# Attention in pairs of heads with one rotary query tile, and the rotary angles two normalisations later

## Chip, cores and metric

One core of one Trainium2 chip runs the whole block once, in float32. The metric is the device time in microseconds of one execution; three executions of the kernel before took 2652.34, 2653.70 and 2655.47 us, median 2653.7.

## What is computed

One decoder block over 2048 tokens of width 1024, cut to what the change touches:

```python
ang = positions[..., None] * inv_freq                 # 32 frequencies
cos, sin = jnp.cos(ang), jnp.sin(ang)
h = rms_norm(x, norm_w) * (1 + scale) + shift         # scale, shift from c @ w_ada
a_val, a_glu, a_gate, cq, ckv, k_pe, b_gate, g_a, g_b = split(h @ w_in)
# convolution branch on a_val, a_glu, a_gate -> y_a
q  = (rms_norm(cq, q_norm_w) @ w_uq).reshape(s, 8, 128 + 64)   # per head: nope, rope
kv = (rms_norm(ckv, kv_norm_w) @ w_ukv).reshape(s, 8, 128 + 128)
q_rope = apply_rope(q[..., 128:], cos, sin)           # [x1*cos - x2*sin, x1*sin + x2*cos]
k_rope = apply_rope(k_pe, cos, sin)                   # one for all heads
scores = (q_nope @ k_nope.T + q_rope @ k_rope.T) * 192 ** -0.5   # causal
o = softmax(scores) @ v
y_b = (o * silu(b_gate)) @ w_attn_out
x = x + gate * ((sigmoid(g_a) * y_a + sigmoid(g_b) * y_b) @ w_out)
return rms_norm(x, final_norm_w)
```

## The kernel before

Each f32 operand of a product is split into a rounded high part (`_hi`) and a remainder (`_lo`), and a product is three matmuls, high by high, high by low and low by high (`split3`, L52 to L54). ScalarE makes most high parts with a copy, VectorE or GpSimd the low parts with a subtraction. The program has three phases. `front_phase` computes the norms, all of `h @ w_in`, the convolution, and the values of all heads. `attention_phase` goes head by head. `output_phase` is not touched.

**Setup, in front_phase.** PE works through weight tiles of 128 columns in four chunks of 512 tokens. Tiles 0 and 1 are the query latents, 2 and 3 the key latents, tile 4 (`KEY`) the rotary key, tile 5 the first of the convolution branch. Latents are normalised chunk by chunk: ScalarE squares (L528), VectorE sums two halves (`sum_squares`, L809), PE takes a mean with a matmul (L1062), ScalarE the root (L533), VectorE the reciprocal and two products (`normalise`, L837 to L840), ScalarE copies the high part (`hi_of`, L546) and squares the next chunk but one, GpSimd the low part (`lo_of`, L714), and SP stores both (L355, L357). Tile 3's chunks ask for the means 3 and 4 (`MEANS`) and for one more root each (`ROOTS`). The nine steps of the angles (L818 to L826) stand on VectorE ahead of the first `normalise`; the two sines (L576, L577) stand on ScalarE ahead of the first `hi_of`; SP stores the table (L389) ahead of the first latents. `split_hi(KEY)` and `split_lo(KEY)` prepare tile 4's weights behind the four chunks. The table is read again for the rotary key (L874 on) once tile 4 is done.

**Attention.** Per head, queries come in four groups of 512, in the order 0, 3, 1, 2 (`ORDER`), each of four blocks of 128. For each block (`S`) PE makes score chunks into a ring of five PSUM banks, five matmuls each (L1502 to L1507) and a mask; VectorE takes the maximum (L1685), ScalarE the exponential into `prob` (`E`, L1619), VectorE sums and inverts, GpSimd scales (L1755). A tile (`T`) is turned by PE (L1522) into one of two banks; ScalarE copies the high part (L1627), VectorE makes the low part (L1708); the product with the values (`PV`, L1537 to L1539) follows two tiles later. T(n) waits until the low part of T(n-2) is done. VectorE multiplies a finished group by the gate (L1716).

The orders are written out by hand in one list of events per head, which each engine walks strictly in turn. The list ends with a tail in which the last 12 tiles stand between 12 projections for the next head: per chunk c, `QN` (query, nope), `QR` (rotary) and `K` (key, nope), each six matmuls of 512 columns into a ring bank. `QR`'s weights are the 64 rotary columns and the same 64 again with their halves swapped, so that its bank holds the rotary part in partitions 0 to 63 and the swapped one in 64 to 127. VectorE's `RA` multiplies them by cosine and signed sine (L1663, L1665) and adds (L1668); ScalarE's `RH` copies the high part to `qr` (L1598), VectorE's `RL` the low part to partitions 64 to 127 (L1673). `VS` splits a quarter of the next head's values (L1607, L1746). A prologue does the 12 projections for the first head without tiles. Seven heads run in a hardware loop, the eighth behind it. A bank is given back in order (`proj_free`), and S0 and S1 take the banks of the last two projections, QR3 and K3.

## Time and profile before

| | before |
|---|---|
| median of three executions | 2653.7 us |
| the profiled execution | 2654.07 us, span 2652.0 us, mean granted clock 0.994 |
| PE busy | 2576.6 us (97%), 12186 matmuls |
| VectorE busy | 1754.9 us (66%) |
| ScalarE busy | 853.6 us (32%) |
| GpSimd busy | 646.8 us (24%) |
| DMA | 305.69 MB, mean 115 GB/s |

A matmul's end is modelled and overlaps the next one's start, so what a matmul costs is read from start to start. DVE is VectorE, ACT ScalarE, POOL GpSimd, SPq SyncE's queue. In square brackets stands how long the engine was idle before the instruction, and which engine, tile and line ended that.

### The profile page before, as it was taken

How to read it: one execution, taken by the hardware profiler on the slowest of the kernel's cores; microseconds unless marked ns; L12 is line 12 of the kernel's file. 1: busy time of each engine (PE TensorE's matmuls, PEld its weight loads, DVE VectorE, ACT ScalarE, POOL GpSimd, SP SyncE). 2: the span in 40 equal slices, each digit the busy share in tenths (PEclk: the TensorE clock that was granted, in tenths of full speed). 3: DMA queues.
4: the chain of work that ended last, by engine and by line, in shares of the span. 5: the costliest groups of instructions: out<-in, count | busy, mean ns of one | idle time of the engine just before them, and what ended most of it. 6: DMA issues, size and time to landing. Idle time of an engine off the chain costs nothing. (4 is left out here: it accounts for less than half of the span.)

```text
span 2652.0 us, 32568 instructions
## 1 busy us (share of the span) xinstructions
PE 2576.6 (97%) x12186; PEld 2122.7 (80%) x12186; DVE 1754.9 (66%) x2069; ACT 853.6 (32%) x1691; POOL 646.8 (24%) x585
## 2 busy tenths in 40 slices
PE   5999999999999999999999999999999999999998
PEld 4777888888888888788787887887887788888887
DVE  5757977989889898666467767767777621223342
ACT  3432111111111111233255565555555521211221
POOL 2222111111111111132033133133233320323422
PEclk9999999999999999999999999999999999999999
DMA  8033312212213121279713112112112265667532
GB/s 303 9 111 106 94 48 73 79 57 84 60 57 89 48 88 48 94 253 333 249 56 109 62 62 105 59 69 101 63 69 80 68 206 163 208 215 225 190 136 79
DMA packets 194240, 305.69 MB, mean 115 GB/s; under 512 B 18169, under 2 KB 111421, under 8 KB 184412
## 3 DMA queue, kind: packets, MB, share of 16 engines
q1 hardware_dynamic: 184412, 279.12, 32.0%
q0 software_dynamic: 5120, 16.78, 1.9%
q10 hardware_dynamic: 4608, 8.39, 0.8%
q8 instruction: 70, 1.15, 0.2%
q14 instruction: 30, 0.25, 0.0%
HBM read 200.97 MB, written 103.28 MB: 115 GB/s over the span
## 5 line engine op out<-in xcount | busy, mean ns | idle before, releaser
L52 PE MATMUL ps_proj<-h_hi,w_hi 128*128 128x512 f32 x1696 | 668.5, 394 | 9.1 <-DVE h_lo L803 6.8
L54 PE MATMUL ps_proj<-h_hi,w_lo 128*128 128x512 f32 x1696 | 661.8, 390 | 0.0
L53 PE MATMUL ps_proj<-h_lo,w_hi 128*128 128x512 f32 x1696 | 661.7, 390 | 0.0
L909 DVE SCALAR_TENSOR_TENSOR acc<-u,taps_t,acc 128x2048 f32<-128x2048 f32 x240 | 628.9, 2620 | 8.5
L52 PEld LDWEIGHTS ps_proj<-h_hi,w_hi 128*128 128x128 f32 x1696 | 319.5, 188 | 77.3 <-issue 7.5
L705 POOL TENSOR_TENSOR w_lo<-raw,w_hi 128x1024 fp32r<-128x1024 f32 x53 | 178.6, 3371 | 819.1 <-ACT w_hi L497 819.0
L53 PEld LDWEIGHTS ps_proj<-h_lo,w_hi 128*128 128x128 f32 x1696 | 319.7, 188 | 67.1 <-issue 1.9
L54 PEld LDWEIGHTS ps_proj<-h_hi,w_lo 128*128 128x128 f32 x1696 | 319.3, 188 | 66.8
L1755 POOL TENSOR_SCALAR prob<-prob,rinv 128x512 f32<-128x512 f32 (+2 forms) x320 | 200.1, 644 | 346.7 <-DVE rinv L1703 346.6
L1708 DVE TENSOR_TENSOR pt_lo<-ps_t,pt_hi 128x512 fp32r<-128x512 f32 (+1 forms) x320 | 194.1, 609 | 93.3 <-ACT pt_hi L1627 89.6
L1627 ACT ACTIVATE pt_hi<-ps_t 128x512 fp32r<-128x512 f32 (+1 forms) x320 | 169.7, 533 | 232.7 <-PE ps_t L1522 232.6
L1685 DVE TENSOR_REDUCE nmax<-ps_ring 128x1 f32<-128x512 f32 (+3 forms) x288 | 174.6, 622 | 96.1 <-PE ps_ring L1507 78.0
L634 ACT ACTIVATE lat<-ps_proj 128x512 f32<-128x512 f32 x120 | 72.0, 600 | 471.3 <-PE ps_proj L54 422.5
L2045 DVE TENSOR_TENSOR o_y<-o_ps,o_g 128x512 f32<-128x512 f32 x63 | 43.2, 690 | 251.6 <-PE o_ps L54 195.6
L1619 ACT ACTIVATE prob<-ps_ring,nbias 128x512 f32<-128x512 f32 (+2 forms) x320 | 195.5, 626 | 37.5 <-DVE nbias L1691 33.0
L52 PE MATMUL o_ps<-o_a_hi,o_w_hi 128*128 128x512 f32 x504 | 196.2, 389 | 0.7 <-PEq L1360 0.7
L54 PE MATMUL o_ps<-o_a_hi,o_w_lo 128*128 128x512 f32 x504 | 196.1, 389 | 0.0
L53 PE MATMUL o_ps<-o_a_lo,o_w_hi 128*128 128x512 f32 x504 | 196.1, 389 | 0.0
L1522 PE MATMUL ps_t<-ident,prob 128*128 128x128 f32 x1088 | 174.1, 276 | 10.1 <-DVE pt_lo L1708 5.3
L1522 PEld LDWEIGHTS ps_t<-ident,prob 128*128 128x128 f32 x1088 | 132.1, 142 | 43.6 <-POOL prob L1755 7.5
L1537 PE MATMUL ps_o<-pt_hi,v_hi 128*128 128x512 f32 (+1 forms) x320 | 141.5, 442 | 0.7 <-DVE bg L1716 0.7
L1502 PE MATMUL ps_ring<-kn_hi,qn_hi 128*128 128x512 f32 (+2 forms) x320 | 125.3, 391 | 8.4 <-ACT prob L1619 5.0
(227 smaller groups left out, 4043.6 us busy)
## 6 DMA issues: line engine op xcount, KB each, us to landing
qlat<-qlat_dram SPq DMA_DIRECT2D x32, 1024.0 KB, 5.5
raw<-in_w_in_dram SPq DMA_DIRECT2D x52, 512.0 KB, 6.4
under_h<-in_w_ada_dram SPq DMA_DIRECT2D x8, 1024.0 KB, 11.3
ga_dram<-lat SPq DMA_DIRECT2D x8, 1024.0 KB, 5.0
gb_dram<-lat SPq DMA_DIRECT2D x8, 1024.0 KB, 5.2
agate_dram<-lat SPq DMA_DIRECT2D x8, 1024.0 KB, 5.0
conv_dram<-acc SPq DMA_DIRECT2D x8, 1024.0 KB, 3.9
v_dram<-v_st SPq DMA_DIRECT2D x4, 2048.0 KB, 9.2
```

The costliest lines, as they stand in the source:

```text
L52: pe.matmul(out, wh, xh, start=first, stop=False)
L53: pe.matmul(out, wh, xl, start=False, stop=False)
L54: return pe.matmul(out, wl, xh, start=False, stop=last)
L705: pool.tensor_tensor(weights(tile)[1][:], raw[tile % 2][:], weights(tile)[0][:].bitcast(F32), ALU.subtract).then_inc(lo_made, 1)
L909: dve.scalar_tensor_tensor(acc[:], u[:, n:n + S], tap(n), acc[:], ALU.mult, ALU.add).then_inc(conv_tap if n < TAPS - 1 else conv_done, 1)
L1522: mm = pe.transpose(ps_t[:, n % 2, b * P:(b + 1) * P], prob[:, x:x + P], k.ident[:])
L1537: pe.matmul(out, v_hi[:, j, :], mh, start=(j == 0), stop=False)
L1619: act.activation(prob[:, x:x + width], ps[:, chunk_no[n, c] % RING, 0:width], ACT.Exp, bias=nbias[:, n:n + 1], accum_out=rsum[:, n, c:c + ...
L1627: act.activation(pt_hi[n % SLOTS][:, s], ps_t[:, n % 2, s], ACT.Copy).then_inc(t_hi, 1)
L1685: ins = dve.tensor_reduce(to, ps[:, chunk_no[n, c] % RING, 0:width], AX.X, ALU.max, negate=True)
L1708: dve.tensor_tensor(pt_lo[n % SLOTS][:, s], ps_t[:, n % 2, s], pt_hi[n % SLOTS][:, s].bitcast(F32), ALU.subtract).then_inc(t_lo, 1)
L1755: pool.tensor_scalar(prob[:, x:x + width], prob[:, x:x + width], rinv[:, n:n + 1], 1.0, ALU.mult, ALU.mult).then_inc(normed, 1)
```

## The change

In attention, heads run in pairs. `QR` is done once for a pair: its weights are the 64 rotary columns of the first head and the 64 of the second, without the swapped copy. For the first head, ScalarE (`QB`) copies the second head's half of the bank to `qb`, and copies the first head's half, swapped, to the new upper half of `rb`; VectorE multiplies by the cosine (`RA`, now one operation) and, after the swap, by the sine, and adds (`RC`). `qb` lies in the part of `prob` that group 1 uses, so it is stored to DRAM and loaded again, plain and swapped, when group 1 of the pair's first head is turned. For the second head, GpSimd multiplies the loaded 128 partitions by the table (`RP`), ScalarE shifts the lower half (`RS`), VectorE adds (`RB`). The loop has three turns of two heads; the last pair stands behind it.

In setup the angles come after two normalisations, the sines and the split of `KEY`'s weights before the third high part, and the store of the table after `KEY`'s load.

```diff
@@ setup, SP @@
-                sp.wait_ge(trig_done, 2)
-                sp.dma_start(k.trig_dram, ang).then_inc(trig_out, 16)
                 store_part(0)
                 store_part(1)
-
                 sp.wait_ge(chunk_mm, 3 * NC_)
                 tile_weights(KEY)
                 gate_load(0)
+                sp.wait_ge(trig_done, 2)
+                sp.dma_start(k.trig_dram, ang).then_inc(trig_out, 16)
                 store_part(2)
@@ setup, ScalarE @@
                 for c in range(NC_):
-                    if 1 <= c < NC_ - 1:
-                        root(c + 1)
+                    if c == 2:
+                        root(2)
+                        split_hi(KEY)
+                        root(3)
+                        turn_angles()
                     hi_of(c)
                     act.wait_ge(part_lo_done, c + 1)
                     evict(2, c)
-                split_hi(KEY)
@@ setup, VectorE; the angle steps move into angles() @@
-                for c in range(NC_):
+                for c in range(2):
+                    normalise(c)
+                    sum_squares(c + 2)
+                angles()
+                for c in range(2, NC_):
                     normalise(c)
-                    if c + 2 < NC_:
-                        sum_squares(c + 2)
@@ attention, order of events @@
+        elif a == 0:
+            ev += [("RP", c) for c in range(NC_)] + [("QN", 0), ("QN", 1)]
+            tiles(2)
+            ev.append(("K", 0))
+            tiles(2)
+            ev.append(("K", 1))
+            for c, then in enumerate([("K", 2), ("K", 3), ("QN", 2), ("QN", 3)]):
+                ev += [("RS", c), ("RB", c)]
+                tiles(1)
+                ev.append(("RH", c))
+                tiles(1)
+                ev += [("RL", c), then]
+                if c == 2:
+                    ev.append(("VS", 0))
         else:
-            ev += [("QN", 0), ("QR", 0), ("RA", 0), ("K", 0), ("RH", 0), ("QN", 1), ("RL", 0)]
+            ev += [("QN", 0), ("QR", 0), ("RA", 0), ("QB", 0), ("RC", 0), ("K", 0), ("RH", 0), ("QN", 1), ("RL", 0)]
             for c in range(1, NC_):
                 if c > 1:
                     ev.append(("QN", c))
                 tiles(1)
-                ev.append(("QR", c))
+                ev += [("QR", c), ("RA", c), ("QB", c)]
                 tiles(1)
                 if c == NC_ - 1:
+                    ev.append(("RC", c))
                     tiles(2)
                     break
-                ev += [("RA", c), ("K", c), ("RH", c)]
+                ev += [("RC", c), ("K", c), ("RH", c)]
@@ attention, SP @@
+                def store_qb(i):
+                    sp.wait_ge(qb_made, (i + 2) * NC_)
+                    sp.dma_start(k.qb_dram, qb[0:ROPE, :]).then_inc(qb_out, 16)
+                def load_qb(i):
+                    sp.wait_ge(qb_out, i * 16 + 16)
+                    sp.wait_ge(t_done, At(i, 0).tile(first_tile[2] + T_CREDIT))
+                    sp.dma_start(qb[0:ROPE, :], k.qb_dram).then_inc(qb_in, 16)
+                    for half in range(2):
+                        at = ROPE + half * HALF
+                        sp.dma_start(qb[at:at + HALF, :],
+                                     k.qb_dram[HALF - half * HALF:ROPE - half * HALF, :]).then_inc(qb_in, 16)
@@ attention, ScalarE @@
+                        elif kind == "RS":
+                            act.wait_ge(rope_step, at.pair(NC_, n + 1))
+                            act.wait_ge(rope_done, at.per(NC_, NC_ + n - 1))
+                            act.activation(ra[n % 2][:], qb[ROPE:P, n * TC:(n + 1) * TC], ACT.Copy).then_inc(rope_shift, 1)
+                        elif kind == "QB":
+                            m = number["QR", n]
+                            act.wait_ge(proj_mm, m + 1 if prol else at.proj(m + 1))
+                            if prol and n == 0:
+                                act.wait_ge(values_stored, 1)
+                            act.activation(qb[0:ROPE, n * TC:(n + 1) * TC], ps[ROPE:P, (N_CHUNK + m) % RING, :], ACT.Copy,
+                                           scale=SCALE).then_inc(qb_made, 1)
+                            act.wait_ge(rope_cos, at.pair(NC_, NC_ + n + 1))
+                            if n or not prol:
+                                act.wait_ge(rope_sum, at.per(NC_, NC_ + n))
+                            for half in range(2):
+                                src = (1 - half) * HALF
+                                act.activation(rb[ROPE + half * HALF:ROPE + (half + 1) * HALF, :],
+                                               ps[src:src + HALF, (N_CHUNK + m) % RING, :], ACT.Copy,
+                                               scale=SCALE).then_inc(swapped, 1)
@@ attention, VectorE @@
                             dve.scalar_tensor_tensor(a[:], bank[0:ROPE, :], SCALE, k.trig[0:ROPE, s],
-                                                     ALU.mult, ALU.mult)
-                            dve.scalar_tensor_tensor(rb[:], bank[ROPE:P, :], SCALE, k.trig[ROPE:P, s],
-                                                     ALU.mult, ALU.mult).then_inc(proj_free, 1)
+                                                     ALU.mult, ALU.mult).then_inc(rope_cos, 1)
+                        elif kind == "RC":
+                            ...
+                            dve.wait_ge(qb_made, at.pair(NC_, NC_ + n + 1))
+                            dve.wait_ge(swapped, at.pair(2 * NC_, 2 * NC_ + 2 * n + 2))
+                            dve.tensor_tensor(rb[0:ROPE, :], rb[ROPE:P, :], k.trig[ROPE:P, s], ALU.mult).then_inc(proj_free, 1)
                             dve.wait_ge(proj_free, m + 1 if prol else at.proj(m + 1))
-                            dve.tensor_tensor(a[:], a[:], rb[:], ALU.add).then_inc(rope_sum, 1)
+                            dve.tensor_tensor(a[:], a[:], rb[0:ROPE, :], ALU.add).then_inc(rope_sum, 1)
+                        elif kind == "RB":
+                            a = ra[n % 2]
+                            dve.wait_ge(rope_shift, at.pair(NC_, n + 1))
+                            dve.tensor_tensor(a[:], qb[0:ROPE, n * TC:(n + 1) * TC], a[:], ALU.add).then_inc(rope_sum, 1)
@@ attention, GpSimd @@
+                        elif kind == "RP":
+                            s = slice(n * TC, (n + 1) * TC)
+                            pool.wait_ge(qb_in, at.pair(48, 48))
+                            pool.tensor_tensor(qb[:, s], qb[:, s], k.trig[:, s], ALU.mult).then_inc(rope_step, 1)
```

The rest of the diff renumbers semaphores for pairs, loads three pieces of weights for a first head (four before) and two for a second, and moves the loads of the query latents with the events.

## Rows read from the trace of the kernel before

**Rows 1.** The page, part 1: busy time (share of span) and instructions of each engine.
```profile
PE 2576.6 (97%) x12186; PEld 2122.7 (80%) x12186; DVE 1754.9 (66%) x2069; ACT 853.6 (32%) x1691; POOL 646.8 (24%) x585
```
**Rows 2.** Waits of PE, whole span: us in total, times, longest.
```profile
PE ps_t L1522 <- DVE pt_lo L1708: 5.3, 9, 0.9
```
**Rows 3.** Timeline of PE: QR0, K0, T4, T5, T12, S0 (start us, us).
```profile
1693.67 0.39 PE L52 MATMUL ps_ring<-qlat,head_w_h 128*128 128x512 f32 x1
1695.05 0.39 PE L52 MATMUL ps_ring<-ckv_hi,head_w_h 128*128 128x512 f32 x1
...
1703.36 0.60 PE L1522 MATMUL ps_t<-ident,prob 128*128 128x128 f32 x4
...
1706.52 0.63 PE L1522 MATMUL ps_t<-ident,prob 128*128 128x128 f32 x4 [0.49 <-DVE pt_lo L1708]
...
1719.73 0.27 PE L1522 MATMUL ps_t<-ident,prob 128*128 128x128 f32 x1
...
1722.39 0.28 PE L1502 MATMUL ps_ring<-kn_hi,qn_hi 128*128 128x128 f32 x1
```
**Rows 4.** Timeline of DVE, same tail: RA0, the gate's product, RA1, lo(T3).
```profile
1695.37 0.67 DVE L1663 SCALAR_TENSOR_TENSOR rope_a<-ps_ring,trig 64x512 f32<-64x512 f32 x1
...
1701.81 0.68 DVE L1716 TENSOR_TENSOR bg<-ps_o,bg 128x512 f32<-128x512 f32 x1
1702.41 0.67 DVE L1663 SCALAR_TENSOR_TENSOR rope_a<-ps_ring,trig 64x512 f32<-64x512 f32 x1
...
1705.68 0.69 DVE L1708 TENSOR_TENSOR pt_lo<-ps_t,pt_hi 128x512 fp32r<-128x512 f32 x1 [0.46 <-ACT pt_hi L1627]
```
**Rows 5.** Timeline of ACT, same tail: RH0, QN1, hi(T2).
```profile
1697.50 0.63 ACT L1598 ACTIVATE qr<-rope_a 64x512 fp32r<-64x512 f32 x1 [0.30 <-DVE rope_a L1668]
1698.04 0.57 ACT L1586 ACTIVATE qn_hi<-ps_ring 128x512 fp32r<-128x512 f32 x1
...
1700.57 0.60 ACT L1627 ACTIVATE pt_hi<-ps_t 128x512 fp32r<-128x512 f32 x1 [1.47 <-PE ps_t L1522]
```
**Rows 6.** The page, part 6: DMA issues, KB each, us to landing.
```profile
qlat<-qlat_dram SPq DMA_DIRECT2D x32, 1024.0 KB, 5.5
```
**Rows 7.** Timelines of POOL and DVE, same tail: VS0 and RL2.
```profile
1714.79 1.28 POOL L1746 TENSOR_TENSOR v_lo<-v_raw,v_hi 128x512 fp32r<-128x512 f32 x1 [17.92 <-ACT v_hi L1607]
...
1714.94 1.68 DVE L1673 TENSOR_TENSOR qr<-rope_a,qr 64x512 fp32r<-64x512 f32 x1
```
**Rows 8.** Timelines in the prologue: SP's first v load, RA1, RA3, S1.
```profile
1305.85 0.83 SPq L1376 DMA_DIRECT2D v_raw<-v_dram  x2
...
1308.67 0.68 DVE L1663 SCALAR_TENSOR_TENSOR rope_a<-ps_ring,trig 64x512 f32<-64x512 f32 x1
...
1317.04 0.67 DVE L1663 SCALAR_TENSOR_TENSOR rope_a<-ps_ring,trig 64x512 f32<-64x512 f32 x1
...
1319.91 0.39 PE L1502 MATMUL ps_ring<-kn_hi,qn_hi 128*128 128x256 f32 x1 [0.60 <-DVE kn_lo L1653]
```
**Rows 9.** Setup: timelines of PE and DVE, and clock (PEclk) by windows.
```profile
69.54 0.50 PE L52 MATMUL ps_proj<-h_hi,w_hi 128*128 128x512 f32 x1 [1.55 <-DVE h_lo L803]
...
142.96 1.10 PE L1062 MATMUL ps_proj<-acc,mean_mat 128*128 128x512 f32 x2 [1.99 <-issue]
...
169.30 0.50 PE L52 MATMUL ps_proj<-h_hi,w_hi 128*128 128x512 f32 x1
...
113.67 1.22 DVE L818 CAST u<-u 128x2048 f32<-128x2048 int32 x1
...
133.28 3.34 DVE L837 RECIPROCAL acc<-acc 128x512 f32<-128x512 f32 x1
...
69.00:72.00 3.00, 2.46 (x13) 2.07 (x14) 2.53 (x5) 3.00 (x7) 0.00 (x0) 1.00 0.00 0
141.00:148.00 7.00, 5.04 (x13) 3.70 (x14) 6.53 (x4) 2.97 (x4) 1.31 (x1) 0.76 0.52 210
```
**Rows 10.** Windows: PE, PEld, DVE, ACT, POOL busy us (count), then PEclk, DMA, GB/s.
```profile
1700.00:1724.00 24.00, 23.25 (x130) 19.24 (x129) 20.08 (x31) 11.23 (x21) 1.36 (x2) 1.00 0.22 78
```

More of the change, by code:

```diff
@@ L1403, in _, with reg, head @@
                         values(0, 1)
-                def head(i, last):
-                    rows = sp.snap(i * P) if not last else i * P
+                store_qb(-1)
+                def reg(x):
+                    return x if isinstance(x, int) else sp.snap(x)
+                def head(i, a, last):
+                    at, rows = At(i, a), reg(i * (2 * P) + a * P)
                     for c in (2, 3):
-                        sp.wait_ge(v_lo_made, At(i).values(c - 2) + 1)
+                        sp.wait_ge(v_lo_made, at.values(c - 2) + 1)
                         sp.sem_inc(passed, 1)
@@ L1424, in head @@
                     for n, g in enumerate(ORDER):
-                        gate(rows, g, i * QB + n)
+                        gate(rows, g, at.per(QB, n))
+                        if g == 1 and a == 0:
+                            load_qb(i)
                         if n == 1 and last:
@@ L1428, in head @@
                                 next_a_in, 16)
[L1429 to L1431 removed]
+                        if n >= QB - 2 and not last and a:
+                            sp.wait_ge(proj_mm, at.proj(order_of(second_body)["QR", n - 2] + 1))
                             q_chunk(n)
+                        if n == QB - 2 and not a:
+                            for c in (2, 3):
+                                sp.wait_ge(proj_mm, at.proj(order_of(first_body)["QN", c - 2] + 1))
+                                q_chunk(c)
                         if g == 1 and not last:
                             for c in (0, 1):
[L1435 removed]
+                                sp.wait_ge(v_lo_made, at.values(c + 2) + 1)
                                 sp.sem_inc(passed, 1)
@@ L1440, in head @@
                             sp.dma_start(k.o_raw[0][:], w_out[:, :, 2 * P:3 * P]).then_inc(next_piece_in, 16)
-                        store(rows, g, i * QB + n)
-                with sp.Fori(0, H - 1) as i:
-                    head(i, False)
-                head(H - 1, True)
+                        store(rows, g, at.per(QB, n))
+                    if a and not last:
+                        sp.wait_ge(qb_in, i * 48 + 48)
+                        store_qb(i)
+                with sp.Fori(0, PAIRS - 1) as i:
+                    head(i, 0, False)
+                    head(i, 1, False)
+                head(PAIRS - 1, 0, False)
+                head(PAIRS - 1, 1, True)
                 sp.wait_ge(o_out, H * QB * 16 + O_OUT_CREDIT)
@@ L1564, in run @@
                             first_unit(at)
-                run(prologue, At(-1), prol=True)
-                with pe.Fori(0, H - 1) as i:
-                    run(body, At(i))
-                run(last_body, At(H - 1))
+                run(prologue, At(-1, 1), prol=True)
+                with pe.Fori(0, PAIRS - 1) as i:
+                    run(first_body, At(i, 0))
+                    run(second_body, At(i, 1))
+                run(first_body, At(PAIRS - 1, 0))
+                run(last_body, At(PAIRS - 1, 1))
             @block.scalar
@@ L1615, in run @@
                                 act.wait_ge(t_done, at.tile(held + T_CREDIT))
+                                if g == 1 and at.a:
+                                    act.wait_ge(rope_done, at.per(NC_, NC_))
+                                elif g == 1:
+                                    act.wait_ge(qb_out, at.pair(16, 16))
                             for c in range(g + 1):
@@ L1627, in run @@
                             act.activation(pt_hi[n % SLOTS][:, s], ps_t[:, n % 2, s], ACT.Copy).then_inc(t_hi, 1)
-                run(prologue, At(-1), prol=True)
-                with act.Fori(0, H - 1) as i:
-                    run(body, At(i))
-                run(last_body, At(H - 1))
+                run(prologue, At(-1, 1), prol=True)
+                with act.Fori(0, PAIRS - 1) as i:
+                    run(first_body, At(i, 0))
+                    run(second_body, At(i, 1))
+                run(first_body, At(PAIRS - 1, 0))
+                run(last_body, At(PAIRS - 1, 1))
             @block.vector
@@ L1756, in run @@
                                                    ALU.mult, ALU.mult).then_inc(normed, 1)
-                run(prologue, At(-1), prol=True)
-                with pool.Fori(0, H - 1) as i:
-                    run(body, At(i))
-                run(last_body, At(H - 1))
+                run(prologue, At(-1, 1), prol=True)
+                with pool.Fori(0, PAIRS - 1) as i:
+                    run(first_body, At(i, 0))
+                    run(second_body, At(i, 1))
+                run(first_body, At(PAIRS - 1, 0))
+                run(last_body, At(PAIRS - 1, 1))
 def output_phase(k):
```

185 lines of the change are left out of this document (100 added, 85 removed).

## The prediction

> **What bounds the kernel now.** I read the page first: TensorE (PE) is busy 97% of the span [rows 1]. The waits of PE come next: in attention it waits only for scraps, the largest of them 5.3 us in nine waits for low halves of turned tiles [rows 2]. So nearly each matmul taken away shortens the run, and each new wait of over about a microsecond lengthens it. Last come the timelines of a head's tail, where one head's last twelve turned tiles (T1 to T12) stand between the projections for the next head. PE works there without a break but for 0.49 us before T5 [rows 3]. Turn T(n) needs the low half (lo) of T(n-2); lo is VectorE's, after ScalarE's high copy (hi). VectorE holds these lo's, all rotary steps and the projections' lo's in one strict queue, and it has little room.
>
> I sum against the profiled execution, 2654.07 us (span 2652.0); the median of the runs, 2653.7, is 0.4 lower.
>
> **First heads of a pair: QR goes.** QR, one projection of 512 columns, takes from its first matmul to K's first 1695.05 - 1693.67 = 1.38 us [rows 3]. A first body has four fewer: 5.5 us. Its tail falls from 30.1 us (1692.28 to S0 at 1722.39; QN0 starts 1.39 before QR0) to 24.6, and the wait at T5 goes too, 0.6 us with PE's restart. What fills VectorE there: per chunk RB, RL, two lo's and a projection's lo, five operations at 0.6 to 0.7 us apart [rows 4], 3.3 us against PE's 3.67 (one projection and two turns with their products, 1.15 each: 1706.52 - 1703.36 less a projection and the wait [rows 3]). But RS on ScalarE, RB on VectorE, RH on ScalarE follow one another, each after the last in a strict queue. Walked with hi 0.60, RH 0.63 [rows 5] and lo 0.69, a chunk takes 3.9 us. Four chunks drift 0.9 us, and S0 comes 5.3 us earlier. Four first bodies: -21.2 us.
>
> The load of `qb` is costed at nothing: it is issued when T of the third group is done (about 1692), and GpSimd has four multiplies. The nearest row for the load is one of 1 MB in one issue, 5.5 us to landing [rows 6]; for a multiply, the v split of the same 128x512 size, 1.28 us [rows 7]. So all four end near 1703 if the three DMAs, 1 MB in sum, land by 1698, while ScalarE wants the first at 1702.4. The cover is 4 us; if it is gone, RS holds ScalarE's hi copies for as long as the load is late. Nothing urgent stands behind this wait in SP's queue: the next query latents are wanted 15 us later. The store of `qb` has about 50 us until group 1 overwrites it: nothing. For RP, the price lies between nothing and the case in the rivals below.
>
> **Second heads of a pair: the swap moves to ScalarE.** VectorE's count stays at three per chunk, but QB puts three copies into ScalarE's queue, two of them after VectorE's RA, and RC waits for these. Copies of 64x512 are the nearest rows: 0.60 to 0.63 us, 0.50 to 0.54 apart when queued [rows 5]; 32 partitions have no row. Half of that is the lower bound, 0.7 each the upper; I take 0.60, since the columns are the same. Behind QB stands the hi copy of the next turn. The walk from the rows:
> - Chunk 0: RA0 ends 1696.04 [rows 4], swaps 1697.2, RC0 (two operations) 1698.6, then K lo, RH0, QN1, RL0. lo(T1) ends 1701.9, 1.1 us later than before.
> - Chunk 1: RA1 then ends 1702.5, the swaps 1703.65. hi(T2), which began at 1700.57 [rows 5], begins 1703.55; its lo ends 1704.85; T4 starts 1705.0 in place of 1703.36 [rows 3]: +1.65.
> - Bank product, RC1, K lo and RH1 follow before lo(T3), which ended 1706.37 [rows 4] and now ends 1708.65: T5 1708.8 in place of 1706.52, +2.3 in sum.
> - Chunk 2 fits. In chunk 3 T9 waits 0.35, and the swaps behind RA3 (1722.0) hold hi(T10) until 1723.0; T12, due 2.3 + 0.4 after its old 1719.73, starts 1724.2, 1.8 later still. S0: 1726.9 in place of 1722.39, **+4.5 us**.
>
> K3's lo binds S1 after it, as now. Three second bodies: +13.5. With the bounds of the swap, 2 to 6 each, so 6 to 18. The last head has no such tail.
>
> **Prologue.** The same chain without turns to cover it. ScalarE's first QB waits until the values are stored (SP sends the first v load at 1305.85 [rows 8]), so RA1 slips from 1308.67 to 1311.0. Then a chunk takes RA 0.7, swaps 1.15, RC 1.4, K, RL and QN lo's 2.1: 5.35 us, against (1317.04 - 1308.67) / 2 = 4.19 [rows 8]. S1, which waits for K3's lo, goes from 1319.91 to 1325.75: +5.9. PE idles some 6 us before S0. An idle of 1.99 us was followed by a granted clock of 0.76 over 7 us, one of 1.55 by 1.00 [rows 9]: 0.76 is a mean of stretches at 1.2 and at 2.4 GHz. I add one such fall and a half, 0.24 x 7 = 1.7 us each: +2.4. Sum +8.3; bounds 4 (the wait hides half) and 11. The setup of the swap's three copies costs nothing else, one-time.
>
> **Setup.** Nine angle operations run from 113.67 to 133.28, ahead of the first normalisation [rows 9]. They hold back the third sum of squares: PE waits 1.99 us for it, then runs at a mean clock of 0.76, and tile 3's last chunk ends at 169.3 [rows 9], 28.3 us after the mean was due (142.96 - 1.99 = 141.0). Without waits its 96 matmuls take 16 times the six of rows 3, 22.1, and the means 0.5. After the move the sums come at 127.9 and 136.8 (reciprocal and two products 4.8 us each, a copy and a square behind them on ScalarE), ahead of 141. The angles end near 155, the second half of the normalisations 164. PE wants what depends on them (the evictions of chunk 2) at 174. Past SP's queue: KEY's weights, first issued after tile 2 (141.2), land near 149; ScalarE's root(3) stands behind their split, due at 158. The table's store, 1 MB, is issued near 159.5 ahead of two stores of latents and is wanted at 185. Each has cover of 8 us or more; with it gone, PE would wait the excess. The gain is 28.3 - 22.6 = 5.7: **-5.7**, bounds -8 and +1. The three DMAs for the first head's weights in place of four: nothing, other loads end last.
>
> **Sum**: -21.2 + 13.5 + 8.3 - 5.7 = -5.1 us, so 2654.07 - 5.1 = 2649.0 us. Halving the number of loop turns removes four of seven loads of ScalarE's table at a head's start; S0's successors wait at most 0.3 us for it. I count it as nothing.
>
> Where a row and a page meet: VectorE's RL, 0.68 us elsewhere, took 1.68 beside GpSimd's v split [rows 7]. The Trainium skill (SBUF — State Buffer, "Who interferes with whom") states that a VectorE instruction with two SBUF inputs contends with a GpSimd one that reads SBUF, and the later one fully blocks. The trace agrees with it. It speaks against RP, which puts four GpSimd multiplies near RB and RL; that is rival 3.
>
> **Rivals.**
> 1. *ScalarE's waits are swallowed.* If the swap copies are short (32 partitions) or hi(T2) and hi(T10) come in time, second tails cost at most 1 us each and the prologue 5: -21.2 + 3 + 5 - 5.7 = -18.9, **2635**. For it: ScalarE is busy 11.2 of 24 us in the tail [rows 10]. Against it: it is the order, not the load, that delays; hi(T2) stands behind a copy that waits for VectorE. 0.20.
> 2. *Slower: the clock falls.* Each second tail has two stalls of 1.65 to 1.8 us, between the idle of 1.55 that kept the clock and that of 1.99 that lost it [rows 9]. Where each loses it, 6 x 1.7 = 10 us, and lo's behind the slower turns take another 0.6 each: -5.1 + 13.8 = +8.7, **2663**. It decides where a stall passes about 2 us, 0.2 above my walk. 0.14.
> 3. *RP comes late.* If `qb` lands after 1702, RP's multiplies meet RB and RL: 1 us [rows 7] for each of up to four, and ScalarE's hi copies wait: first tails give back 3.5 each. -5.1 + 14: **2663**, slower. For: three DMAs on 64 and 32 partitions have no row. Against: 4 us of cover. 0.08.
> 4. *The setup gives nothing*, since the angles' delay turns up at KEY's evictions or in root(3): -5.1 + 5.7 = +0.6, **2654.7**, no change. 0.12.
> That the change doesn't do what it says can't be: 96 matmuls are gone from the program of 12186 on PE [rows 1].
>
> **How the numbers follow.** Forecast 0.46, its own range 2642 to 2656 (from the bounds of the swap and the prologue, which will hardly all fall one way). About 0.2% of 2653.7 us, 5.3 us, is what a measurement of this kernel can tell from no change, and the forecast lies just inside that border: I split it 0.23 faster, 0.21 same, 0.02 slower. Faster 0.23 + 0.20 = 0.43; same 0.21 + 0.12 = 0.33; slower 0.02 + 0.14 + 0.08 = 0.24. The range takes in rival 1 to its edge and most of 2 and 3: 2636 to 2662.
>
> **What the profile of after would show.** First tails: S0 24.8 us after QN0, RS waiting for nothing. Second tails: PE's waits on `pt_lo` at T4, T5 and T12, 1 to 2 us each, ended by VectorE, and ScalarE idle before its swaps until RA. Prologue: S1 27 us after QN0 in place of 21.3. Setup: no wait before the third mean, KEY's first matmul near 163.4. PE without low clock between 141 and 163. The prediction is wrong if second tails show no `pt_lo` waits (then 1), if clock falls stand in them (2), or if `rope_step` holds ScalarE (3).

## The result and the profile after

The changed kernel takes 2663.9 us (median of 6 runs, 2659.8 to 2664.8) against 2653.9 for the kernel before (6 runs, 2652.3 to 2655.5): ratio 1.0034, 95% interval 1.0024 to 1.0044. It is slower by 9.9 us, where I had forecast 2649.0, faster by 4.7. The time lies 1.9 us above the range.

The profiled execution is the fastest of the six, 2659.8 us (span 2658.0, against 2652.0 before), so the trace can account for 6.0 of the 9.9 us. The other 4 are scatter between executions, and no row explains them. The clock doesn't either: its mean was 0.988 in the profiled execution and 0.989 to 0.992 in the five slower ones.

Of the page of the changed kernel, the first lines and the two instruction queues (queue and kind: packets, MB, share of 16 engines):

```profile
span 2658.0 us, 32198 instructions
PE 2557.7 (96%) x12090; PEld 2105.8 (79%) x12090; DVE 1722.5 (65%) x2037; ACT 883.5 (33%) x1751; POOL 666.1 (25%) x601
...
q8 instruction: 101, 1.65, 0.3%
q14 instruction: 61, 0.49, 0.1%
```

PE lost its 96 matmuls, and its share of busy time fell [rows 1]: it waits more than before. The waits of PE in the changed kernel (engine, line, what ended the wait: us in total, times, longest):

```profile
PE ps_o L1609 <- DVE bg L1826: 10.2, 4, 3.1
PE ps_t L1594 <- DVE pt_lo L1818: 8.9, 8, 1.8
PE ps_ring L1574 <- DVE rope_b L1771: 6.2, 1, 6.2
PE ps_ring L1574 <- DVE qr L1783: 3.3, 1, 3.3
```

Three of these four have no counterpart of such size before [rows 2]: the wait for `bg` (the product of the attention output with the gate, which empties the only bank `ps_o`), the one in the prologue for `rope_b`, and 3.3 us at the first scores (S0) after the loop's jump back.

**Where the trace's 6.0 us lie.** I cut both spans at the same places, at PE's start of setup tiles 2 and 5 and at corresponding points of each head:

| stretch | before to after, us | forecast |
|---|---|---|
| until setup tile 2 | -2.6 (differs from run to run) | 0 |
| setup, tile 2 to 5 | -5.1 | -5.7 |
| prologue | +7.3 | +8.3 |
| four first bodies, 101.0 each before, 95.7 to 96.0 now | -20.1 | -21.2 |
| three second bodies, 101.0 before; 112.0, 111.8, 107.4 now | +28.2 | +13.5 |
| after the last head | -1.7 | 0 |

The row of the second bodies is 14.7 us off, the others together -3.6. The third second body, after which the loop is left without a jump back, costs 6.4 us more than before, and the first two 4.5 to 4.7 more than the third: 3 x 6.4 = 19 us for the tails and 9 for the two jumps.

The last row is no gain of the change. In the last head PE waits for GpSimd's scaling of `prob` in both kernels. The wait in the kernel before and its windows row for the 12 us behind it (window, its length, busy us and instructions of the engines, clock, DMA share, GB/s), then that row of the changed kernel:

```profile
2101.61 1.12 PE L1522 MATMUL ps_t<-ident,prob 128*128 128x128 f32 x4 [3.20 <-POOL prob L1755]
```
```profile
2101.60:2113.60 12.00, 11.33 (x50) 9.62 (x51) 4.75 (x7) 4.08 (x7) 3.61 (x3) 0.63 0.31 88
```
```profile
2109.60:2121.60 12.00, 11.14 (x62) 9.78 (x63) 6.04 (x9) 4.94 (x9) 3.62 (x3) 0.86 0.28 87
```

The wait is the same, 3.2 us. Behind it the mean clock was 0.63 before and 0.86 in the changed kernel's profiled execution, and nothing of the change stands there.

**A first head's tail.** PE's timeline (start, duration, what; in brackets the idle time before it and what ended it), first QN0, then the last product and S0:

```profile
1388.97 0.39 PE L52 MATMUL ps_ring<-qlat,head_w_h 128*128 128x512 f32 x1
...
1413.74 0.38 PE L1609 MATMUL ps_o<-pt_hi,v_hi 128*128 128x256 f32 x1 [0.51 <-DVE pt_lo L1818]
...
1414.95 0.28 PE L1574 MATMUL ps_ring<-kn_hi,qn_hi 128*128 128x128 f32 x1
```

26.0 us from QN0 to S0, where the kernel before took 30.1 in each tail. The forecast was 24.8. PE waits at three places, none of them forecast: 0.51 and 0.20 us for low halves at the last products, and 0.37 us at T1 for GpSimd's scaling. T1 now stands behind two projections, where it stood behind four:

```profile
1392.27 0.66 PE L1594 MATMUL ps_t<-ident,prob 128*128 128x128 f32 x4 [0.37 <-POOL prob L1870]
```

The GpSimd and ScalarE timelines show that `qb` comes in time: the multiplies begin when the load lands, and RS (L1678) has no bracket, so it waited for nothing:

```profile
1395.94 5.03 POOL L1853 TENSOR_TENSOR prob<-prob,trig 128x512 f32<-128x512 f32 x4 [2.39 <-DMA prob<-qb_dram]
```
```profile
1399.87 0.63 ACT L1678 ACTIVATE rope_a<-prob 64x512 f32<-64x512 f32 x1
```

**A second head's tail.** ScalarE, VectorE and PE of the changed kernel in the same stretch, an engine to a fence:

```profile
1492.95 0.59 ACT L1685 ACTIVATE prob<-ps_ring 64x512 f32<-64x512 f32 x1
1495.23 1.20 ACT L1692 ACTIVATE rope_b<-ps_ring 32x512 f32<-32x512 f32 x2 [1.69 <-DVE rope_a L1763]
1496.45 0.60 ACT L1726 ACTIVATE pt_hi<-ps_t 128x512 fp32r<-128x512 f32 x1
```
```profile
1494.53 0.67 DVE L1763 SCALAR_TENSOR_TENSOR rope_a<-ps_ring,trig 64x512 f32<-64x512 f32 x1
1497.08 0.69 DVE L1818 TENSOR_TENSOR pt_lo<-ps_t,pt_hi 128x512 fp32r<-128x512 f32 x1 [1.88 <-ACT pt_hi L1726]
1497.69 0.68 DVE L1826 TENSOR_TENSOR bg<-ps_o,bg 128x512 f32<-128x512 f32 x1
```
```profile
1484.87 0.39 PE L52 MATMUL ps_ring<-qlat,head_w_h 128*128 128x512 f32 x1
...
1494.69 0.63 PE L1594 MATMUL ps_t<-ident,prob 128*128 128x128 f32 x4
1498.42 0.59 PE L1609 MATMUL ps_o<-pt_hi,v_hi 128*128 128x512 f32 x1 [3.10 <-DVE bg L1826]
...
1499.66 1.06 PE L1594 MATMUL ps_t<-ident,prob 128*128 128x128 f32 x4
...
1519.23 0.33 PE L1594 MATMUL ps_t<-ident,prob 128*128 128x128 f32 x1 [1.77 <-DVE pt_lo L1818]
...
1525.37 0.32 PE L1574 MATMUL ps_ring<-kn_hi,qn_hi 128*128 128x128 f32 x1 [3.26 <-DVE qr L1783]
```

Read across the engines. ScalarE copies `qb`, then stands 1.69 us for VectorE's RA1, copies the two swapped halves, and only then makes hi(T2). VectorE, which holds the strict order, stands 1.88 us for hi(T2), makes lo(T2), and only then the gate's product. PE has turned T3 and wants to start PV(T1), the first product of the next group, into `ps_o`; it stands 3.10 us until the gate's product has emptied it. At the last turn, T12, PE waits 1.77, and at S0 3.26.

The granted clock after these waits (window, its length, busy us and instructions of the engines, clock, DMA share, GB/s):

```profile
1498.00:1506.00 8.00, 7.58 (x31) 6.14 (x32) 5.70 (x9) 2.68 (x5) 0.00 (x0) 0.79 0.54 198
1516.00:1525.00 9.00, 4.34 (x24) 3.22 (x22) 6.13 (x10) 3.97 (x9) 1.26 (x1) 1.00 0.09 31
1525.00:1533.00 8.00, 7.63 (x35) 6.40 (x36) 2.99 (x9) 3.65 (x9) 1.44 (x3) 0.79 0.96 252
```

After the wait of 3.10 us PE runs part of the eight microseconds at the lower level, 1.2 GHz; a mean of 0.79 costs (1 - 0.79) x 8 = 1.7 us. It is 0.79 behind the same wait in the other two second tails too. The wait of 1.77 us is inside the second window, and the clock keeps 1.00. After the 3.26 us at the jump another 1.7 us are lost. At the second jump the order is another: the clock falls at T12 already (0.83 over 1722 to 1732), PE waits only 1.47 us for S0, and loses 1.7 us more behind it, in sum about the same.

### The profile page after: what moved, and what is told of

The parts are those of the page before. It is cut to its first block and busy times, and to the rows that moved or that the text cites. A ratio compares the mean times of both kernels' runs of the same rounds, so it can differ in the third digit from the quotient of the medians.

```text
span 2658.0 us, 32198 instructions
## 1 busy us (share of the span) xinstructions
PE 2557.7 (96%) x12090; PEld 2105.8 (79%) x12090; DVE 1722.5 (65%) x2037; ACT 883.5 (33%) x1751; POOL 666.1 (25%) x601
## 3 DMA queue, kind: packets, MB, share of 16 engines
q8 instruction: 101, 1.65, 0.3%
```

## Experiments

The changed kernel was timed in another batch than the experiments, in whose batches the kernel before took 2654.1 to 2654.8 us. The intervals of the ratios make about 3.7 us of uncertainty in a difference between two changed forms of different batches, so the tails of the traces carry more than such differences do.

Below, tail means QN0 to S0 on PE's timeline, by kernel: first tail, second tail with a jump back behind it, and the last second tail without one.

| kernel | prologue | first | second, jump | second, no jump | ratio to before |
|---|---|---|---|---|---|
| before | 19.9 | 30.1 | | 30.1 | 1 |
| changed | 26.0 | 25.8 to 26.0 | 40.5, 40.3 | 37.0 | 1.0034 |
| e1 setup only | 20.1 | 30.1 | | 30.1 | 0.9972 |
| e3 before, two heads a turn | 20.1 | 30.1 | 32.2, 32.1 | 30.1 | 1.0006 |
| e4 pairs, no loop | 26.0 | 25.9 to 26.5 | | 35.8 to 38.8 | 1.0008 |
| e7 no loop on PE | 26.1 | 26.1 to 26.7 | | 35.6 to 38.3 | 1.0012 |
| e8 gate's product first | 26.0 | 25.8 to 26.0 | 38.1, 38.0 | 35.0 | 1.0016 |
| e2 copies behind turn | 26.0 | 25.8 to 25.9 | 35.5, 35.5 | 32.1 | 0.9990 |
| e5 swap first | 22.1 | 25.8 to 26.0 | 35.5, 35.6 | 32.1 | 0.9974 |
| e6 swap first, no loop | 22.1 | 25.8 to 26.3 | | 32.4 | 0.9938 |

**The setup part alone.** The kernel before with only the part of the change in setup:

```diff
-                sp.wait_ge(trig_done, 2)
-                sp.dma_start(k.trig_dram, ang).then_inc(trig_out, 16)
                 store_part(0)
...
                 gate_load(0)
+                sp.wait_ge(trig_done, 2)
+                sp.dma_start(k.trig_dram, ang).then_inc(trig_out, 16)
...
-                for c in range(NC_):
+                for c in range(2):
                     normalise(c)
-                    if c + 2 < NC_:
-                        sum_squares(c + 2)
+                    sum_squares(c + 2)
+                angles()
+                for c in range(2, NC_):
+                    normalise(c)
```

> The kernel before with the setup part of the change alone; attention stays as before. In the profile of the changed kernel the stretch from tile 2's first matmul to tile 5's first matmul is 5.1 us shorter. If that is all that the move does, this runs 4 to 6 us faster than before (ratio 0.998). If the move only shifts a wait behind setup, into the convolution or the attention, it is within 1 us of before.

Measured: 2648.7 us (7 runs) against 2654.7, ratio 0.9972 [0.9961, 0.9984], so -6.0 us. The trace shows how: PE has no wait before the third mean, and the clock that stood at 0.76 over 141 to 148 us [rows 9] stays whole until `KEY` is begun:

```profile
141.00:163.00 22.00, 22.00 (x96) 17.84 (x95) 21.76 (x11) 8.89 (x8) 6.18 (x2) 1.00 0.38 101
```

So the setup part is worth what was forecast. If the two parts add, the attention part of the change costs 2663.9 - 2653.9 + 6.0 = 16 us.

**Two heads per loop turn, without pairs.** The kernel before, its loops on all engines turned half as often with twice the body:

```diff
-                with pe.Fori(0, H - 1) as i:
-                    run(body, At(i))
+                with pe.Fori(0, H // 2 - 1) as i:
+                    run(body, At(i * 2))
+                    run(body, At(i * 2 + 1))
+                run(body, At(H - 2))
                 run(last_body, At(H - 1))
```

> The kernel before with two heads in each turn of the loop (three turns, two heads behind it), nothing else changed. In the changed kernel PE starts S0 3.3 and 1.5 us late at the loop's two jumps back and not at its exit, with every semaphore that S0 waits for long given. If the length of the loop's body makes this, here too PE idles 1 to 3 us at two places, S0 of the third and fifth head, and the kernel is 2 to 8 us slower than before. If something of the pairs makes it (the store of the second head's rotary half, the longer SP queue), this is within 1 us of before.

Measured: 2656.7 us against 2654.7, ratio 1.0006 [0.9997, 1.0015]. The time alone shows no change, but the trace is plain. PE's timeline at the first jump back:

```profile
1523.31 0.32 PE L1504 MATMUL ps_ring<-kn_hi,qn_hi 128*128 128x128 f32 x1 [1.98 <-issue]
```
```profile
1523.00:1530.00 7.00, 6.69 (x31) 5.64 (x32) 3.60 (x8) 2.93 (x8) 1.83 (x3) 0.76 0.71 211
```

"issue" means that PE waited for nothing that the profile shows, no engine and no transfer. It stands 1.98 us there (1.92 at the second jump), with a clock of 0.76 behind it, while the kernel before has no idle time at its S0 [rows 3]. Nothing of the change is in this kernel but the length of the body, so that length alone costs 2 us a jump and the clock: the two stretches from QN0 to QN0 with a jump in them take 103.7 and 103.8 us, against 101.0.

Why is the total hardly longer? The other stretches take 100.5 to 100.7. In the kernel before, ScalarE loads its table for the exponential once per head, seven times; here, as in the changed kernel, three times. The load in a head of the kernel before:

```profile
1524.22 1.28 ACT L1619 ACT_TABLE_LOAD   x1 [2.33 <-DVE nbias L1685]
```

PE reaches its 60th matmul after S0 12.6 us later with such a load and 12.15 without, so each load is worth 0.5 us. Two jumps at 2.7 us each less four times 0.5 make 3.4 us; the span of this trace is 3.2 longer than that of the kernel before.

The transfers show what is special at a jump. Of the view of the DMA between 1420 and 1940 us, which covers five heads, the kernel before has one queue and no packet of instructions:

```profile
q1 hardware_dynamic: 18912, 42.21, 22.9%
```

The same stretch with two heads per turn, then the changed kernel:

```profile
q8 instruction: 27, 0.44, 0.4%
q14 instruction: 28, 0.23, 0.1%
```
```profile
q8 instruction: 26, 0.43, 0.3%
q14 instruction: 28, 0.23, 0.1%
```

So with one head per turn no code is fetched again, and with two heads it is fetched in every turn. The 3.3 us before S0 at the changed kernel's first jump (1522.11 to 1525.37) contain such packets:

```profile
q8 instruction: 1, 0.02, 2.1%
q14 instruction: 2, 0.02, 1.2%
```

Without a loop (e4, below) the code is fetched too, 21 and 16 packets over the same 520 us, but none between 1722 and 1732, around S0 at 1728.64, and PE doesn't wait there. I read this as PE waiting for the code that follows the jump; no row names the packet that it waits for. In one head's period PE executes 544 matmuls and 544 weight loads, 1088 in sum; in a pair of the changed kernel 1064 of each, 2128 in sum.

The Trainium skill (Advanced Engine Details and Errata, "ISA Cache") gives TensorE 128 KB of instruction cache and 256 instructions to 16 KB. An estimate from that page is 2048 instructions, which lies between the 1088 and the 2128. That agrees with the trace, but no run here shows where the limit is.

**The pairs without a loop.** The changed kernel, its loop written out on all engines, so that no engine jumps back:

```diff
-                with pe.Fori(0, PAIRS - 1) as i:
+                for i in range(PAIRS - 1):
                     run(first_body, At(i, 0))
                     run(second_body, At(i, 1))
```

> The changed kernel with the three turns of the attention loop written out on every engine. If the jumps back cost PE 3.4 and 1.6 us, and the low clock after them some 2 to 4 more, this is 5 to 9 us faster than the changed kernel (2655 to 2659), and S0 follows the last product directly at all heads. If the idle comes from elsewhere, it is still there and the time is the same within 1 us.

Measured: 2657.4 us, ratio 1.0008 [0.9999, 1.0017], so 6.4 us less than with the loop; about 1 us of it is an estimate for two table loads fewer (one in place of three). No wait stands at S0 in this trace; the waits for `bg` and `pt_lo` are as in the changed kernel, 10.0 and 9.1 us in sum. Its three second tails tell something else: 37.3, 35.8 and 38.8 us long, with the same wait of 3.10 us in each. The clock behind the first and the second of them:

```profile
1502.00:1510.00 8.00, 7.83 (x34) 6.42 (x34) 5.61 (x10) 2.92 (x6) 0.00 (x0) 0.79 0.54 197
1706.00:1714.00 8.00, 7.47 (x38) 6.06 (x39) 6.40 (x10) 3.93 (x7) 0.00 (x0) 1.00 0.56 197
```

Where the clock stayed whole the tail took 35.8 us, where it fell once 37.3. In the third it fell twice: it is 0.89 over 1908 to 1924 us, behind the wait of 3.10, and 0.83 over 1924 to 1934, where T12 waits 1.8 us, 3.5 us lost in sum. One wait thus doesn't always have the same price: 5.7 us over the 30.1 of before are the waits, and each fall adds 1.4 to 1.7.

**The loop written out on PE alone.** The same edit, on PE and nowhere else.

> The changed kernel with the loop written out on PE alone; ScalarE, VectorE, GpSimd and SP keep it. With the loop off all engines PE's late S0 (3.3 and 1.5 us) was gone and the kernel ran 6.4 us faster than the changed one. If it is PE's own jump that costs, this gives the same, 2656 to 2659. If PE is late because another engine is (SP or VectorE at their jumps), S0 or the scores behind it still wait and the gain is under 3 us.

Measured: 2658.1 us, ratio 1.0012 [1.0003, 1.0021]. Its second tails scatter in the same way: 36.9 us at 0.79 over 8 us behind the wait, 38.3 at 0.57, 35.6 at 1.00. S0 isn't late, and a smaller wait follows for ScalarE's probabilities, which is late after its own jump:

```profile
1530.09 0.50 PE L1574 MATMUL ps_ring<-kn_hi,qn_hi 128*128 128x512 f32 x1 [0.70 <-ACT prob L1718]
```

So 5.8 of the 6.4 us go with PE's own jump; the 0.6 between this run and the last is within the noise. The wait that the profile of the changed kernel puts down to "DVE qr L1783" was no wait for VectorE: S0 needs RL2, and that ran from 1512.67 to 1514.33, 11 us before S0.

**The gate's product ahead of lo(T2).** The changed kernel with one exchange in VectorE's order in the second body; ScalarE and PE are as they were:

```diff
+                at_t2 = second_body.index(("QB", 1)) + 1
+                dve_second = second_body[:]
+                dve_second[at_t2:at_t2 + 2] = dve_second[at_t2:at_t2 + 2][::-1]
                 with dve.Fori(0, PAIRS - 1) as i:
                     run(first_body, At(i, 0))
-                    run(second_body, At(i, 1))
+                    run(dve_second, At(i, 1))
```

> The changed kernel, but in the second head's tail VectorE multiplies the bank by the gate (L1826) ahead of lo(T2) instead of behind it. Theory A, the single bank: the product no longer waits for ScalarE's late hi(T2), so it comes 1.9 us sooner than RA1's successor does now; TensorE's wait for it falls from 3.1 us to 0.5 to 0.9, too short for a clock fall, and each second tail from 40.4 us (37.0 where no jump back follows) to about 33.5 to 34.5 without the jump, what my walk had forecast; a wait of up to 1 us for pt_lo may come up two turns later. Three tails at 3 to 4 us less: about 2652 to 2655 us. Theory B, ScalarE's order alone: the wait only changes its name, from the product to pt_lo (PV and the next turns need lo(T2) anyway); tails stay at 36 to 37, the run at 2661 to 2664. The waits at the two jumps stay at about 3.3 and 1.5 to 3.3 us under both.

Measured: 2658.2 us (10 runs), ratio 1.0016 [1.0007, 1.0026], 5.7 us less than the changed kernel; each second tail is 2.0 to 2.5 us shorter, 35.0 us without the jump. The waits and the clock in PE's rows:

```profile
1498.58 0.50 PE L1609 MATMUL ps_o<-pt_hi,v_hi 128*128 128x512 f32 x1 [0.53 <-DVE bg L1826]
...
1500.55 0.66 PE L1594 MATMUL ps_t<-ident,prob 128*128 128x128 f32 x4 [1.01 <-DVE pt_lo L1818]
...
1503.95 0.63 PE L1594 MATMUL ps_t<-ident,prob 128*128 128x128 f32 x4 [0.66 <-DVE pt_lo L1818]
```
```profile
1498.00:1503.00 5.00, 3.45 (x17) 2.49 (x16) 3.18 (x5) 3.24 (x7) 0.00 (x0) 1.00 0.32 109
```

Both theories hold in part, and neither to its number. Of the 3.10 us for the product, 0.53 remain, and 1.67 come back as waits for low halves, which ScalarE's order still delays: 0.9 us of waiting are gone. Behind none of the three did the clock fall, in any of the three second tails, and that is the larger part, 1.1 to 1.6 us by difference. My expectation of 3 to 4 us a tail had left the returning waits out. The excess over the kernel before that remains, 35.0 - 30.1 = 4.9 us, is what is left of ScalarE's order with the clock whole, and it is almost the +4.5 that I had walked.

**The copies behind the turn.** In the second body, QB comes one turn later in each chunk, in the first of them behind T2:

```diff
-                ev += [("QR", c), ("RA", c), ("QB", c)]
+                ev += [("QR", c), ("RA", c)]
                 tiles(1)
+                ev.append(("QB", c))
```

> The changed kernel with QB moved behind the turned tile that follows QR in second bodies (order QR, RA, T, QB, RC), so that ScalarE's high copy of that tile, VectorE's low half and the product with the gate no longer stand behind copies that wait for RA. If this order makes the loss, PE's wait of 3.1 us for the gate's product falls to 0.5 to 1.5 us and the 1.8 us at the last turn goes, second bodies are 4 to 6 us shorter each, and the kernel gains 12 to 18 us against the changed one (2646 to 2651). If it is the amount of work on ScalarE and VectorE that binds, the waits only move and it gains under 4 us.

Measured: 2652.2 us, ratio 0.9990 [0.9981, 0.9999], 11.7 us less than the changed kernel. The product is waited for 1.13 us, not 3.10, and the wait at T12 is gone:

```profile
1499.49 0.50 PE L1610 MATMUL ps_o<-pt_hi,v_hi 128*128 128x512 f32 x1 [1.13 <-DVE bg L1827]
```

A second tail falls by 5 us, from 37.0 to 32.1. So the place of the copies in ScalarE's queue, ahead of a hi copy that PE needs, is the cause of five of the seven microseconds, the clock's fall behind it included.

**The swap first.** On top of that, the two swap copies go ahead of VectorE's RA and of the copy to `qb`, in the second tails and in the prologue. Of their own chunk they need only PE's projection. RA now waits for them, where they waited for RA before:

```diff
-            ev += [("QN", 0), ("QR", 0), ("RA", 0), ("QB", 0), ("RC", 0), ("K", 0), ("RH", 0), ("QN", 1), ("RL", 0)]
+            ev += [("QN", 0), ("QR", 0), ("QB", 0), ("RA", 0), ("RC", 0), ("K", 0), ("RH", 0), ("QN", 1), ("RL", 0)]
...
-                            act.wait_ge(rope_cos, at.pair(NC_, NC_ + n + 1))
...
-                            dve.wait_ge(proj_mm, m + 1 if prol else at.proj(m + 1))
+                            dve.wait_ge(swapped, at.pair(2 * NC_, 2 * NC_ + 2 * n + 2))
```

> As the run with the copies behind the turn, and besides in QB the two swapping copies come first, need only PE's projection, and VectorE's RA waits for them (order QR, T, QB, RA, RC): nothing on ScalarE waits for VectorE's RA any more. If ScalarE's wait for RA is what remains of the loss, PE's wait for the gate's product (1.13 us with copies behind the turn) falls under 0.6, the tail of a second head without a jump is 31 us or less (32.06 there, 37.0 in the changed kernel), and the prologue, where one projection chunk takes 5.44 us, takes 4.6 per chunk, so QN0 to S0 is 22 to 23 us in place of 26.0. In sum 3 to 6 us faster than with the copies behind the turn alone, 2646 to 2649. If the queue on VectorE is what remains, the tail and the prologue stay as they are.

Measured: 2647.6 us against 2654.8, ratio 0.9974 [0.9965, 0.9983]. The prologue's tail falls from 26.0 to 22.1 us. The second tail stays at 32.1, against my expectation: the product is waited for 0.46 us instead of 1.13, but 0.50 and 0.64 for low halves come up in its place:

```profile
1493.70 0.50 PE L1610 MATMUL ps_o<-pt_hi,v_hi 128*128 128x512 f32 x1 [0.46 <-DVE bg L1826]
1497.69 0.63 PE L1595 MATMUL ps_t<-ident,prob 128*128 128x128 f32 x4 [0.50 <-DVE pt_lo L1818]
...
1514.20 0.38 PE L1610 MATMUL ps_o<-pt_hi,v_hi 128*128 128x256 f32 x1 [0.64 <-DVE pt_lo L1818]
1518.36 0.32 PE L1575 MATMUL ps_ring<-kn_hi,qn_hi 128*128 128x128 f32 x1 [3.25 <-issue]
```

The last row is the jump, here named "issue" as it should be.

A form in which neither waits for the other wasn't tried.

**Both repairs.** The swap first, and the loop written out on all engines.

> The last one with the loop's turns written out on every engine. Two jumps back cost PE 3.4 us each where the loop stands, so 7 us less than the last run and with the low clock after them up to 10: 2637 to 2642, the fastest of all, about 0.5% under the kernel before. If the time of the jumps comes back as a wait elsewhere (the next scores wait for ScalarE and VectorE anyway), under 3 us.

Measured: 2636.9 us (5 runs) against 2654.8, ratio 0.9938 [0.9924, 0.9951], 10.7 us less than with the loop and 27 less than the changed kernel. It beats both kernels: without its two faults the changed kernel gains 16 to 18 us. Not all of that is the pairs'. 6.0 us are the setup part's, and 3 us are an estimate for six table loads fewer (one in place of seven, 0.5 each), which the kernel before would gain as well with its loop written out; that kernel wasn't run. Some 8 us are left for the pairs.

## Why the prediction was wrong

**Setup: right.** -5.7 forecast; -5.1 in the trace, -6.0 timed alone. The third mean waits for nothing and the clock stays whole, as written. `KEY`'s first matmul was due at 163.4 (163.6 by the forecast's own sum) and came at 161.81, in an execution whose tile 2 starts 2.6 us earlier. The work of tile 3 was undersized: from the third mean (138.25) to `KEY` PE runs 23.6 us without a break, where 22.6 were forecast.

**First bodies: right in size, in part by luck.** -21.2 forecast, -20.1 measured. S0 comes 26.0 us after QN0, not 24.8, so the tail gives 4.1 us. The body still saves 5.1: K3's lo no longer binds S1 behind it, and the next head has no table load, which the forecast counted as nothing and which is worth 0.5 us, 2 us over the four first bodies. Half a microsecond that was left out thus covered part of a tail that was walked too short. RS waits for nothing. The load of `qb` lands in 4 to 6 us as its nearest row suggested [rows 6], and GpSimd takes 5.03 us for four multiplies, 1.26 each against the 1.28 of the row used [rows 7]. Rival 3, RP too late, fell. Its contention is real but small: VectorE's first RB took 0.97 us beside the multiplies where its neighbours took 0.68. The drift of 0.9 us over four chunks didn't come, since the chunks follow PE's own pace (3.66 us); in its place stand the waits of 0.37 us at T1 and of 0.51 and 0.20 at the last products, with PE's restart behind each.

**Prologue: right in mechanism and size.** +8.3 forecast, +7.3 measured. The chunk takes 5.44 us where 5.35 were walked (RA at 1303.35, 1308.79 and 1314.22), S1 stands 27.3 us after QN0 (27 forecast), and PE waits 6.16 us ahead of S0 (6 forecast). Of the 7.3 us, 6.0 stand at S1, where 5.9 were walked, and 1.3 behind it, where 2.4 had been put in for the clock. The clock fell once, while PE was still idle, and part of the fall cost nothing: it is 0.70 over the 7 us behind S0.

**Second bodies: the step that failed.** +13.5 forecast, +28.2 measured, for two reasons.

1. *The walk of chunk 1 left out who waits for the gate's product.* I wrote that bank product, RC1, K lo and RH1 follow before lo(T3), and priced that for T5 alone. But `ps_o` is one bank, and PE's next product after T3, PV(T1), can't start until the gate's product has read it. VectorE's strict order puts that behind lo(T2), which ScalarE had made late. In the kernel before, PV(T1) stood here in the tail of [rows 3]:

```profile
1702.55 0.50 PE L1537 MATMUL ps_o<-pt_hi,v_hi 128*128 128x512 f32 x1
```

My walk had lo(T2) end at 1704.85, so with 0.68 for the product [rows 4] its own numbers put PV(T1) at 1705.5, 3.0 us late, and T4 as late behind it, not 1.65. In the trace T4, due 1.65 us late, came 3.7 late (1499.66 - 1484.87 = 14.8 us after QN0, where it was 11.1 before), T5 then waited for nothing, and from there the tail ran nearly as walked: T9 waited 0.6 us where I had 0.35, T12 1.77 where I had 1.8. With the product moved ahead, T4 is 1.9 us late (12.96 us after QN0) and the tail 4.9 us longer than before, against 4.5 walked. The mechanism was right and the term mis-sized: of the 7.0 us, 5.6 are waits (the tails whose clock stayed whole took 35.6 to 35.8) where 4.5 were walked, and about 1.4 are the clock, which falls behind the one wait of 3.1 us into which the bank joins the delays, and not behind the three shorter ones of e8. Undoing it alone was worth 2.0 to 2.5 us a tail and 5.7 us of the time.

2. *The loop was counted as nothing.* I looked at what the longer body saves (loads of ScalarE's table at a turn's start) and not at what it costs. The kernel before shows no idle time at its jumps, but that row is of a body half as long and says nothing of this one. I should have put a range on it, as I did for other operations without a row. At the first jump it is 3.3 us of PE and 1.7 of clock behind it, at the second about as much in other portions: 9 us in the trace, 6.4 in the timed comparison. Of the 9, about 1 us is the table load behind each jump, which the third second body is spared: it is 7.0 us longer in its tail and 6.4 as a whole.

By the timed comparisons the two make 5.7 + 6.4 = 12.1 of the 14.9 us between forecast and median. The rest is within the scatter between executions, and I have no cause for it.

**The rivals.** Rival 2 gave 2663, close to the result, by luck: three falls of 1.4 to 1.7 us in the tails make about a third of the 14.7 us by which the second bodies missed. It had the clock fall at both stalls of every second tail. It fell at the first, which was 3.1 us long and not 1.65, and at T12 in one tail of three. The trace of before had a row for a stall of that size, the 3.20 us of its last head with 0.63 over 12 us behind it, and the prediction didn't use it. The rival's condition was about right: the stalls of 1.8 us at T12 kept the clock but for two tails, one of the changed kernel and one of e4, those of 1.98 and 1.92 at the jumps of e3 lost it, and of nine of 3.1 us seven lost it. Rivals 1 and 4 fell: hi(T2) wasn't in time, and the setup gave its gain. Half of rival 1's argument was wrong as well: copies of 32 partitions aren't shorter, two take 1.20 us.

The range was too narrow because it was built from known mechanisms only; it had no part for a changed loop.

## What to carry to other kernels

When an operation is put into a strict queue behind a wait, follow not only the next turn but each product, bank and buffer that the same queue releases later, and ask which of them has a single copy: here the one bank `ps_o` made one wait of 3.1 us out of smaller ones, and the clock fell behind it. Try to put an operation that needs only PE ahead of those that wait for another engine: it gave 3.9 us in the prologue here, and nothing in the second tails. And when a change makes a loop's body longer, price the jump: if its code no longer stays on the core, the profile shows packets of instructions in every turn and "issue" at the first instruction behind the jump, and then a loop written out can be the faster one.

## What the runs showed of the hardware

- A jump back to a body of 1064 matmuls and as many weight loads idles PE for 2.9 to 3.4 us (1.5 where the clock had fallen before); of 1088 (two heads of the kernel before) 1.9 to 2.0 us; of 544, nothing. What makes 3.3 of 2.0 with about the same count stays open.
- The profile can name an engine for such a wait ("DVE qr L1783") that had long been done; only the same wait in its sister kernels, where it is called "issue", and its absence with PE's loop written out tell what it is.
- Idle times of 1.8 us at T12 left the granted clock at 1.00 in most tails of the changed kernel, e4 and e7, and twice gave 0.83 over 10 us; 1.98 us gave 0.76 over the 7 us behind it. The nine idle times of 3.10 us (changed kernel, e4, e7) gave 0.79 over 8 us in most cases, once 0.57, and twice 1.00. The 3.2 us of the last head were followed by a fall in all ten kernels, 0.63 over 12 us in the kernel before and 0.86 in the changed one. What decides between them stays open.
- A load of ScalarE's table takes 1.28 us, and one at a head's first exponential delayed PE by 0.5 us.
- ScalarE's copy of 32 partitions by 512 from the matmul bank takes 0.59 us, as do 64 and 128 partitions (0.60 each).
